# Values projected by token, the gates' activations split in halves, and the removal keys' sum of squares as two float32r products, in one inference step of a hybrid encoder

## The reference, cut to what matters

```python
rcols = (rms_norm(h) @ w_in)[RWKV columns]            # r, k, v: 512 columns each, decay and iclr: 64 each
prev = concat([state_or_zero, rcols[:, :-1]])         # the row of the token before
xs = rcols + (prev - rcols) * mix                     # token shift
r, k, v, wd, ad = split(xs)
kk = heads(k * k_k)                                   # removal keys
kk = kk * rsqrt(max(sum(kk * kk, -1), 1e-24))         # per head of 64
y, S = wkv_scan(r, decay, k, v, kk, a, state0)        # S[v, k], one update per token
y = (group_norm(y) + (r * k * r_k).sum(-1) * v) * silu(g)
```

## Time and profile before

| what | us |
|---|---|
| median of 3 runs | 1772.4 (1764.19 to 1772.84) |
| the profiled execution | 1771.13, of which its span 1769.3 |
| PE busy | 1707.2 (96%) |
| DVE, ACT, POOL busy | 828.6, 799.4, 417.3 |

### The profile page before, as it was taken

The page is one execution under the profiler, slowest core; times in us unless marked ns, Lnnn a source line. Parts: engine busy times, 40 slices in busy tenths (PEclk is TensorE's granted clock), DMA queues, the critical chain, the costliest instruction groups (busy, mean ns, idle before and its releaser), DMA issues. The chain is left out here.

```text
span 1769.3 us, 48548 instructions
## 1 busy us (share of the span) xinstructions
PE 1707.2 (96%) x21338; PEld 1398.7 (79%) x21338; DVE 828.6 (47%) x1198; ACT 799.4 (45%) x1656; POOL 417.3 (24%) x282
## 2 busy tenths in 40 slices
PE   6999999999998999999889999999999999889999
PEld 5778888888887888999667777787777777667787
DVE  4345444444444311223446565555565556643432
ACT  5556666665655322223434444444444444423420
POOL 3332221122110000000213544334454334320000
PEclk9999999999999999999889999999999999899999
DMA  6322211112134412214311212212212213466652
GB/s 228 110 73 81 59 52 68 56 57 74 44 109 174 154 61 87 85 61 146 112 48 52 72 52 66 67 52 63 60 52 75 58 53 108 143 252 230 205 176 87
DMA packets 119138, 170.88 MB, mean 97 GB/s; under 512 B 39568, under 2 KB 78992, under 8 KB 118672
## 3 DMA queue, kind: packets, MB, share of 16 engines
q1 hardware_dynamic: 109280, 152.76, 26.8%
q10 hardware_dynamic: 9648, 15.01, 2.3%
HBM read 113.21 MB, written 55.06 MB: 95 GB/s over the span
## 5 line engine op out<-in xcount | busy, mean ns | idle before, releaser
L652 PE MATMUL a_ps_proj<-a_w_hi,a_x_hi 128*128 128x512 f32 x384 | 155.8, 406 | 0.0
L652 PE MATMUL a_ps_proj<-a_w_hi,a_x_lo 128*128 128x512 f32 x384 | 150.2, 391 | 0.0
L652 PE MATMUL a_ps_proj<-a_w_lo,a_x_hi 128*128 128x512 f32 x384 | 149.6, 390 | 0.0
L1056 DVE SCALAR_TENSOR_TENSOR j_out<-j_ps,j_rest,j_part 128x512 f32<-128x512 f32 (+2 forms) x65 | 41.9, 645 | 220.4 <-ACT j_last_cols L1004 170.0
L562 DVE SCALAR_TENSOR_TENSOR a_stage<-a_ps_s,a_new_bias 128x256 f32<-128x256 f32 x64 | 27.2, 424 | 229.0 <-PE a_ps_s L679 229.0
L2222 PE MATMUL r_ps_gate<-gate_w_hi,gate_x_hi 128*128 128x512 f32 x272 | 116.5, 428 | 4.6 <-PEq L66 3.4
L2222 PE MATMUL r_ps_gate<-gate_w_lo,gate_x_hi 128*128 128x512 f32 x272 | 116.4, 428 | 0.0
L2222 PE MATMUL r_ps_gate<-gate_w_hi,gate_x_lo 128*128 128x512 f32 x272 | 116.3, 428 | 0.0
L1002 ACT ACTIVATE j_part<-j_last_cols,j_shift_in 128x1 f32<-128x1 f32 x65 | 19.2, 296 | 212.8 <-PE j_ps L1081 212.8
L1862 DVE TENSOR_TENSOR r_w_mat<-r_ps_w,consts 128x512 f32<-128x512 f32 x83 | 57.3, 691 | 106.0 <-PE r_ps_w L2106 106.0
L337 POOL TENSOR_TENSOR a_xT<-a_xT,a_row 128x1024 f32<-128x1024 f32 x17 | 40.4, 2374 | 251.6 <-DMA a_row<-scratch_rstd 241.0
(11 more groups left out here) (383 smaller groups left out, 4690.2 us busy)
## 6 DMA issues: line engine op xcount, KB each, us to landing
a_xT<-in_x_T SPq DMA_DIRECT2D x17, 512.0 KB, 3.6
scratch_xT<-a_xT SPq DMA_DIRECT2D x17, 512.0 KB, 2.6
raw<-scratch_xT SPq DMA_DIRECT2D x17, 512.0 KB, 4.6
scratch_gates<-r_gate_out SPq DMA_DIRECT2D x34, 256.0 KB, 2.4
z_gate<-scratch_gates SPq DMA_DIRECT2D x17, 512.0 KB, 4.3
xs<-scratch_xs_T SPq DMA_DIRECT2D x15, 576.0 KB, 4.3
a_x<-in_x_prompt SPq DMA_DIRECT2D x16, 512.0 KB, 4.5
scratch_xs_T<-j_out ACTq DMA_DIRECT2D x39, 192.0 KB, 1.9
```

The source lines that it names most:

```text
L652: mm = nc.tensor.matmul(ps_proj[:], a[n % 2][:, k, :], w[:, k, g * AW:(g + 1) * AW], start=(k == 0 and i == 0), stop=(k == KT - 1 and i == 2))
L1056: last = nc.vector.scalar_tensor_tensor(out=out[j][:, 0:n], in0=ps[j][:, 0:n], scalar=rest[:, c:c + 1], in1=part[j][:, 0:n], op0=ALU.mult, ...
```

## The change

1. The values (blocks 8 to 11) leave the transposed projection. For them PE now takes the tokens as the stationary side, tile by tile, and the four value blocks as the moving side (512 columns), so a value tile comes out by token: 17 units of 24 products. They stand between the blocks of the same group, in turn with them (`SHIFT_UNITS`).
2. Their token shift is done by token: ACT copies PSUM into `v_raw`; SP stores it to `scratch_v_raw` and, when that has landed, loads it back one row lower into `v_prev`; POOL subtracts, multiplies with mix and adds (three instructions of 128x512); SP stores the result in four pieces to `scratch_v_tok`. There are two `v_raw` and one `v_prev`.
3. In the recurrence SP loads `v_tok` and `v_swap` of a tile from there (three DMAs per tile), and the turn, its two PSUM jobs and ACT's two copies are gone. The shifted tile is loaded without the value blocks.
4. `kk * kk` goes to POOL; ACT rounds the square to float32r (`kk_hi`), DVE subtracts (`kk_lo`), and PE sums both with a float32r copy of the ones. `kk_sum` moves ahead of the state's update (key 30.05 for 31.4).
5. ACT and POOL split the gates' activations in two halves of four k blocks; PE waits for the first half at its first product and for the second at its thirteenth.
6. The constants' load now waits until all value tiles are stored, and SP's loads in the last group stand between the value tiles' DMAs.

```diff
+SIZES = (4, 4, 3, 3, 3)
+XS_BLOCKS, V_BLOCKS = (0, 1, 2, 3, 4, 5, 6, 7, 12), (8, 9, 10, 11)
+def shift_units():
+    units = []
+    for g, n in enumerate(SIZES):
+        blocks, values = [(g, c, None) for c in range(XS_TILES)], [(g, None, a) for a in range(n)]
+        at = 5 if g == 0 else 0
+        units += blocks[:at]
+        for i in range(n):
+            units += [blocks[at + i], values[i]]
+        units += blocks[at + n:]
+    return units
...
 # shift projection, SP
+            def turn_rows(t):
+                sp.wait_ge(v_copied, t + 1)
+                sp.dma_start(v_rows(t, 0), v_raw[t % 2]).then_inc(v_raw_stored, 16)
+                wait(sp, v_mixed, t)
+                sp.wait_ge(v_set_up, 32)
+                sp.wait_ge(v_raw_stored, 16 * (t + 1))
+                sp.dma_start(v_prev[:], v_rows(t, 1)).then_inc(v_prev_loaded, 16)
...
+                    if a is not None:
+                        t = tile_of(g, a)
+                        turn_rows(t)
+                        store_v(t)
+                        if t == DEC:
+                            sp.wait_ge(v_stored, 64 * (DEC + 1))
+                            sp.dma_start(r_consts[:], io["shape_consts"]).then_inc(shared.params_loaded, 16)
...
+                    if g == GROUPS and c in (2, 3, 5):
+                        load_gate_w({2: 2, 3: 3, 5: 4}[c])
...
 # shift projection, ACT
+                    if a is not None:
+                        t = tile_of(g, a)
+                        if g == 0:
+                            act.wait_ge(x_lo_ready, KT + 4 * (t % 2) + 4)
+                        wait(act, v_stored, 64 * (t - 1))
+                        nc.scalar.activation(v_raw[t % 2], ps[j][:], ACT.Copy).then_inc(v_copied, 1)
...
+                    if g == GROUPS and m in GATE_AT:        # GATE_AT = (0, 4, 7, 9)
+                        split_gate_w(GATE_AT.index(m))
...
 # recurrence, PE
-                yield 31.4
-                need(pe, t, "kk_sq")
+                yield 30.05
+                pe.wait_ge(head_sums_ready, 1)
+                need(pe, t, "kk_hi", "kk_lo")
                 ps, done = free_bank(t, "kk_sum")
-                nc.tensor.matmul(ps[:], const("head_ones"), kk_sq[:], start=True, stop=True).then_inc(done, 1)
-                yield 35.3
-                turn_two(t, "v_tok", xs[u][:, 8:12], "v_swap", xs[u][:, 8:12])
+                nc.tensor.matmul(ps[:], head_sums[:], kk_hi[:], start=True, stop=False)
+                nc.tensor.matmul(ps[:], head_sums[:], kk_lo[:], start=False, stop=True).then_inc(done, 1)
...
 # recurrence, SP
+            def front(t, u, mode):
+                yield 12
+                wait(sp, ready["ps_y"], t - 1)
+                wait(sp, ready["v_bonus"], t - 1)
+                sp.wait_ge(shared.v_stored_by_token, 64 * (TILES + 1))
+                sp.dma_start(v_tok[u][:].rearrange("p m d -> p (m d)"), io["v_tok"][t]).then_inc(v_loaded[u], 16)
+                for g in range(2):
+                    sp.dma_start(v_swap[u][half(g)].rearrange("p m d -> p (m d)"), io["v_tok"][t, half(1 - g), :]).then_inc(v_loaded[u], 16)
```

More of the change, by code:

```diff
@@ L82, with shift_stores @@
 SHIFT_W0, GT = 4, 4
+SIZES = (4, 4, 3, 3, 3)
+XS_BLOCKS, V_BLOCKS = (0, 1, 2, 3, 4, 5, 6, 7, 12), (8, 9, 10, 11)
+XS_TILES = len(XS_BLOCKS)
+def shift_units():
[8 more added lines that the diff above has]
+    return units
+SHIFT_UNITS = shift_units()
+def shift_stores(j, before):
+    return sum(q % 2 == j for q, (g, c, a) in enumerate(SHIFT_UNITS[:before]) if c is not None)
 class Shared:
@@ L873, in prompt_cols, with units, splits, tile_of @@
             return (SIZES[g] - (g == GROUPS)) * P
-        def blocks(g):
-            for c in range(SHIFT_TILES):
-                i = g * SHIFT_TILES + c
-                yield c, i % 2, i // 2
-        def done(g, j):
-            return ((g + 1) * SHIFT_TILES + 1 - j) // 2
+        W_ORDER = XS_BLOCKS[:6] + V_BLOCKS + XS_BLOCKS[6:]
+        AHEAD = [[2], [3], [4, 5], [6, 7], [8, 9], [10], [11], [12]]
+        first_unit = [next(q for q, unit in enumerate(SHIFT_UNITS) if unit[0] == g) for g in range(len(SIZES))] + [len(SHIFT_UNITS)]
+        def units(g):
+            for q in range(first_unit[g], first_unit[g + 1]):
+                yield q, q - first_unit[g], SHIFT_UNITS[q][1], SHIFT_UNITS[q][2], q % 2, q // 2
+        def done(g, j):
+            return (first_unit[g + 1] + 1 - j) // 2
+        GATE_AT = (0, 4, 7, 9)
+        def splits(g, m):
+            if g == 0:
+                return {2: (0,), 3: (1,), 4: (2,), 5: (3,), 6: (4, 5), 7: (6, 7)}.get(m, ())
+            return (m - 3,) if 0 <= m - 3 < KT else ()
+        def tile_of(g, a):
+            return first(g) + a
+        def mixes(q):
+            return sum(unit[1] is not None and i % 2 == q % 2 for i, unit in enumerate(SHIFT_UNITS[:q]))
+        def values(q):
+            return sum(unit[2] is not None for unit in SHIFT_UNITS[:q])
         def by_stream(ap, size):
@@ L1020, in _ @@
+                    if q > 0:
+                        store(q - 1)
+                    if g < GROUPS:
+                        for k in splits(g, m):
+                            split_x(g + 1, k)
+                    if g == GROUPS and m in GATE_AT:
+                        split_gate_w(GATE_AT.index(m))
+                    if g == GROUPS and m == 2:
                         split_gate_x()
-            store(GROUPS, SHIFT_TILES - 1)
+            store(len(SHIFT_UNITS) - 1)
         @block.vector
@@ L1502, in back @@
                                      states[:, :, now, :].rearrange("p c b d -> p c (b d)")).then_inc(stored, 16)
-            tiles(sp, nothing, back, mix, tail, gates, first_gates, out)
+            tiles(sp, front, back, mix, tail, gates, first_gates, out)
             for j in range(2):
@@ L1637, in mix @@
                 yield 21.7
-                need(act, t, "kk", "acc")
-                nc.scalar.activation(kk_sq[:], kk[:], ACT.Square).then_inc(ready["kk_sq"], 1)
+                need(act, t, "kk")
+                was_written(act, t, "kk_sum")
+                nc.scalar.activation(kk_hi[:], kk[:], ACT.Square).then_inc(ready["kk_hi"], 1)
             def front(t, u, mode):
```

322 lines of the change are left out of this document (199 added, 123 removed).

## The result

The changed kernel takes 1749.96 us in the median of 4 runs (1747.64 to 1753.65), the kernel before 1771.55 in the same job (1764.19 to 1772.84). The ratio is 0.9886, with a 95% interval of 0.9865 to 0.9908: 1.1% faster. The forecast was 1741 with a range of 1731 to 1758. The profiled execution took 1753.65 us with a span of 1751.5, which is 17.8 less than before.

What follows compares the result with a forecast made beforehand. PE was taken to bound the recurrence, busy 590.89 of 600 us. Loops 31.5, head 3 and projection 1 us off, 4.5 on at the projection's end: 31 off, 1741 us; range 1731 to 1758, likeliest case 0.65.

Steps and rivals of the forecast that it cites:

- rival B: End of the projection: the value tiles' chain takes 14 to 17 us, the recurrence starts much later; 1753 us, chance 0.12.
- the end of the projection: Value tiles' chain of 11.5 us on SP makes the last gate weights late, before the recurrence: 4.5 us on.
- the head: Start of the recurrence: turn and float32 kk_sum of tiles 0 and 1 go, a DVE subtraction comes: 3 us off.
- The seam: Between two loops of the recurrence: kk_sum, turn and wait save 2.1 us a loop, 31.5 over fifteen loops.
- The turn: At the seam on PE: the turn of the values goes, saving 1.11 us a loop.
- The wait: At the seam: PE's wait for DVE's reading of kk_sum, in front of the turn, goes: 0.48 us a loop.
- what could be late next: At the seam moved forward: checked whether the next tile, its transpose, gates' activations or new squares would come late; cost nothing.
- thinnest place: In front of the gates: first half of the split activations ready at about 1200.1, a cover of 0.1 us only.
- Rival A: Loops: gates' halves or DVE's first product of a tile come late, 1.4 us a loop, not 2.1; 1751, chance 0.11.
- kk_sum, 0.59 forecast: At the seam on PE: two float32r products at 0.46 us replace one of 1.05, saving 0.59 a loop.
- The projection on PE: Value blocks in the shift projection: 93.2 us of PE products become 92.2, 1 us off.
- the rule's worst case: POOL in the value tiles: all three products stretched to 1.78 us by the shared ports, chain 13.0, end 4.5 us later.

Runs made afterwards that it cites:

- b2: The kernel before with the turn of the values cut to one of its eight pairs of products; ratio 0.9913 to the kernel before.
- b3: The kernel before with kk_sum moved ahead of the state's update, still one float32 product; 1820.8 us, ratio 1.0274.
- h1: The changed kernel with the gates' activations in one piece again, not in halves; 1781.3 us, ratio 1.0054 to the kernel before.
- p1: The changed kernel with POOL's two subtractions for the gates' activations replaced by fills of zeros; ratio 0.9816 to the kernel before.
- w4: The changed kernel with DVE's reading of kk_sum ahead of the state's two instructions at the seam; ratio 0.9825 to the kernel before.
- k1: The changed kernel with kk_sum as one float32 product of the square, at its new place; ratio 0.987 to the kernel before.
- w5: The changed kernel with DVE's reading of kk_sum ahead of the state's update and kk_sum as one float32 product; median 1745.4 us.
- m1: The changed kernel without POOL's multiplication by the mix in the value tiles, two instructions in place of three; ratio 0.984 to the kernel before.

## Why the prediction was right in its range and not in its case

The time lies in the range of 1731 to 1758, and 1 us above the 1733 to 1749 of the likeliest case. What happened is rival B, for which I had worked out 1753 and given 0.12. I had forecast 31 us off; the medians gave 21.6 and the profiled executions 17.8. The missing 13.2 us of the profiled ones are 6.9 in the end of the projection, 1.0 in PE's part of it, 1.8 in the head, 0.8 in the loops and 2.8 in the rest.

**The seam, right in sum, in part by luck.** I took 2.1 us a loop and 31.5 in all; the loops gave 30.7, but 3.3 of these are the four slow loops of the kernel before, and a regular loop gave 1.8. The forecast had read its 37.5 us as a mean over these loops. The seam fell by 2.33 (2.18 forecast). The turn in it is the 1.11 us forecast; b2 shows that it was PE time. The wait is read from PE's rows: the read-out is followed after 0.34 us in place of 0.95, so 0.61 went for 0.48. No run takes the wait out alone; b3 was meant to and lost more elsewhere. Of the 2.33, 0.52 was given back in the long part.

**The step "what could be late next" failed.** I followed PE's list and the gates' activations, found a cover of 0.1 us there, and called it the thinnest place. It held, by 0.06 us (POOL's first half ends at 1196.27 and the gates start at 1196.33); h1 shows that it was needed. I did not walk DVE's own queue at the seam: by moving `kk_sum` ahead of the state's products I delayed these, and with them the state's two instructions, the reading of `kk_sum` and `w_mat` behind them. p1 gives 0.47 us per loop back and w4 0.32. Rival A had named "DVE's first product of a tile" and took 1.4 a loop for it; it came late by less than that. Nor did I see that a wait of PE can cost more than its length: in h1 and b3 the granted clock fell behind it.

**kk_sum, 0.59 forecast.** Between its start and that of the state's products lie 0.55 us for the pair (1193.61 to 1194.16) and 0.95 in k1: 0.40, not 0.59. In the changed kernel it bought nothing; only with DVE's queue mended did 0.26 a loop remain.

**The head, 3 forecast, 1.2 measured.** From the second `kk_sum` to the first level it fell from 5.5 to 3.2 us, the 2.4 forecast. The part before grew by 1.0 us, where I had the turn of tile 0 off and 0.7 for the subtraction on. There PE's wait of 2.8 us in front of the turn went, but a wait of 1.7 us for `kk_lo` is new, and PE stands idle for 4.1 us in front of the next gates, for 1.2 before. In k1 and w5 the head is 40.2 and 40.8 us although the wait for `kk_lo` is still there (1.3 and 2.1 us), so that wait alone is not the reason; why they are shorter stays open. **The projection on PE**: 1 us off forecast (with 0.226 us a product, where 40 us by 178 are 0.225, which changes nothing); the executions with the new order scatter by more (305.3 to 308.0 us; with the old one 305.5 to 306.8), so nothing is shown.

**The end of the projection, the term that was mis-sized.** 4.5 forecast (4.3 by its own working, 60.4 less 56.1), 11.4 measured. The row that I picked for the store's landing was 2.0 us, from a store of equal size in another stage; here the store was followed by its load after 4.0, 5.1 and 5.0 us, beside the loads of weights and tiles. The chain without its other issue was 13.6 and 14.5 us in place of 11.5, and the constants' issue came 46.7 us behind the first store instead of some 37. Of these 9.5 us the three stores are 8. The weights landed 1.6 us sooner than I took (6.0 for 7.6) and the first store stood 1.0 earlier: 6.9 us are left, which is the difference to the 11.4. That each us counts about three times held (m1). POOL's three products took 1.48, 1.29 and 1.28 in the last group's first tile: the 1.78 each that I gave as the rule's worst case did not come there. The stretch came elsewhere, on DVE, where I had not looked.

## What to carry to other kernels

When an instruction is moved or made shorter on the bounding engine, walk the other engines' queues at that place too: what stands in order behind the instruction that now starts later, and who waits for the last of them. Price a chain of transfers by the landing times of the same stage, with the same neighbours, and never by the smallest row; before moving a large load, ask whose store it will fly beside. A saving on the bounding engine shows only once the next queue is mended: the same float32r pair was worth 0 and 0.26 us a loop. And look at the granted clock behind every new wait of PE: in h1 and b3 it added 1.45 and about 0.7 us a loop to waits of 1.8 and 3.1 us.

## What the runs showed of the hardware

DVE's scaling of the state, whose two inputs lie in SBUF, waits out a POOL subtraction that began first. It takes 0.43 us alone. It took 1.21 behind a POOL subtraction of 1.27 us, 0.81 when POOL had begun 0.4 us earlier relative to it (1191.70 in k1), and 2.30 behind one of 2.34 us (b3). In each it ended about 0.3 us behind POOL. In h1 the scaling began 0.14 us ahead of POOL's subtraction (1172.03 and 1172.17) and took 0.43. DVE instructions with one input from PSUM are not stretched: the state's addition takes 0.42 us in k1, where POOL's subtraction runs beside the whole of it (1191.99 to 1192.41), and in the changed kernel the reading of `kk_sum` and `w_mat` take 0.68 us beside POOL's second half. The Trainium skill says this (SBUF — State Buffer, Who interferes with whom): DVE with two SBUF inputs contends with GpSimd instructions that read SBUF and not with those that only write, and the order of issue decides who is blocked. The trace agrees on the two inputs and on the order. That POOL's reading makes the difference no run here shows, since p1's fill was too short to tell. A forecast from that rule would have needed the order of two starts that lie 0.35 us apart, which the change itself decided.

PE's granted clock fell to the lower level, 1.2 GHz, for 3.4 us behind waits of 1.80 us in seven of the 15 loops of h1 and behind waits of 3.09 us in all 15 of b3. Why it fell in seven loops of h1 and not in the seven others with a wait of 1.8 us these runs do not show.
